# Moving four weight buffers by 32 bytes within each partition

## What is computed

```python
for i in range(DEPTH):
    h = rmsnorm(x, norm_mix_pre[i])
    m = ssd_mixer(h, ...) if i % 2 == 0 else rglru_mixer(h, ...)
    x = x + rmsnorm(m, norm_mix_post[i])
    h = rmsnorm(x, norm_ffn_pre[i])
    f = conv_ffn(h, ffn_w_up[i], ffn_conv_w[i], ffn_conv_b[i], ffn_w_down[i])
    x = x + rmsnorm(f, norm_ffn_post[i])
...
```

## Time and profile before

| what | before |
|---|---|
| median of 3 runs | 1814.41 us |
| the profiled execution's own time | 1813.63 us |
| its span, first to last instruction | 1811.3 us |
| TensorE matmul busy | 1763.0 us, 97% |
| TensorE weight load busy | 1642.5 us, 91% |
| VectorE busy | 1292.1 us, 71% |
| ScalarE busy | 1012.9 us, 56% |
| granted TensorE clock, mean | 0.997 of full speed |

### The profile page before, as it was taken

One profiled execution on the slowest core, in us unless ns is written; L12 is line 12 of the kernel. 1 busy time (PEld: TensorE's weight loads), 2 busy tenths in 40 slices (PEclk: granted clock), 3 DMA queues, 4 the chain that ended last, 5 costly groups with the idle time before them and its releaser, 6 DMA issues. The chain is left out here.

```text
span 1811.3 us, 37750 instructions
## 1 busy us (share of the span) xinstructions
PE 1763.0 (97%) x15197; PEld 1642.5 (91%) x15197; DVE 1292.1 (71%) x1997; ACT 1012.9 (56%) x1582; POOL 33.5 (2%) x56
## 2 busy tenths in 40 slices
PE   7999999999999999999999999999999999999999
PEld 7996788989979699899889999999998999999999
DVE  6838777777778987777778766775557876686555
ACT  6645565555576765555566654554455665455443
POOL 0000000000000000000000001000000000100000
PEclk9999999999999999999999999999999999999999
DMA  8540566677675565665636430545553542044553
GB/s 332 185 162 1 197 224 245 251 264 292 255 296 179 217 246 197 246 243 199 255 116 207 143 115 3 217 180 190 200 191 140 166 162 93 26 163 165 198 196 117
DMA packets 45285, 338.32 MB, mean 187 GB/s; under 512 B 5104, under 2 KB 5360, under 8 KB 6896
## 3 DMA queue, kind: packets, MB, share of 16 engines
q1 hardware_dynamic: 38736, 277.89, 42.8%
q0 software_dynamic: 4992, 52.43, 7.4%
q10 hardware_dynamic: 1440, 6.33, 0.9%
HBM read 333.48 MB, written 1.05 MB: 185 GB/s over the span
## 5 line engine op out<-in xcount | busy, mean ns | idle before, releaser
L679 DVE TENSOR_TENSOR w_lo<-raw,w_hi 128x1024 fp32r<-128x1024 f32 x526 | 638.7, 1224 | 355.0 <-ACT w_hi L670 341.4
L670 ACT ACTIVATE w_hi<-raw 128x1024 fp32r<-128x1024 f32 x526 | 553.4, 1060 | 547.0 <-PE unit L701 327.1
L699 PE MATMUL unit<-h_hi,w_hi 128*128 128x256 f32 x2528 | 705.7, 279 | 6.2 <-ACT keep L2028 1.9
L700 PE MATMUL unit<-h_lo,w_hi 128*128 128x256 f32 x2528 | 701.3, 277 | 0.0
L701 PE MATMUL unit<-h_hi,w_lo 128*128 128x256 f32 x2528 | 701.2, 277 | 0.0
L699 PEld LDWEIGHTS unit<-h_hi,w_hi 128*128 128x128 f32 x2528 | 476.1, 188 | 11.3 <-issue 3.2
L700 PEld LDWEIGHTS unit<-h_lo,w_hi 128*128 128x128 f32 x2528 | 474.9, 188 | 1.3
L701 PEld LDWEIGHTS unit<-h_hi,w_lo 128*128 128x128 f32 x2528 | 475.6, 188 | 0.0
L699 PE MATMUL acc<-mv_hi,w_hi 128*128 128x256 f32 x640 | 177.5, 277 | 0.4 <-DVE mv_lo L827 0.2
L700 PE MATMUL acc<-mv_lo,w_hi 128*128 128x256 f32 x640 | 177.3, 277 | 0.0
L701 PE MATMUL acc<-mv_hi,w_lo 128*128 128x256 f32 x640 | 177.3, 277 | 0.0
(11 more groups left out here) (420 smaller groups left out, 2127.8 us busy)
## 6 DMA issues: line engine op xcount, KB each, us to landing
raw<-w_in SPq DMA_DIRECT2D x263, 1024.0 KB, 4.8
ada_ring<-ada_in POOLq DMA_DIRECT2D x32, 1536.0 KB, 10.5
h<-rows_in ACTq DMA_DIRECT2D x5, 512.0 KB, 3.7
late<-keep POOLq DMA_DIRECT2D x8, 256.0 KB, 4.3
keep<-gates_in ACTq DMA_DIRECT2D x1, 1280.0 KB, 9.9
par<-par_in ACTq DMA_DIRECT2D x1, 1036.0 KB, 11.9
x<-x_in SPq DMA_DIRECT2D x2, 512.0 KB, 4.9
out<-x SPq DMA_DIRECT2D x4, 256.0 KB, 2.3
```

The costliest lines, as they stand in the source:

```text
L670: act(half(w_hi, c, k), raw[c % RAW][:, CW // 2 * k:CW // 2 * (k + 1)], ACT.Copy).then_inc(S("high_parts"), 1)
L679: tt(half(w_lo, c, k), raw[c % RAW][:, CW // 2 * k:CW // 2 * (k + 1)], half(w_hi, c, k).bitcast(f32), ALU.subtract).then_inc(S("chunk_spli ...
L699: mm(out, w, m, start=first, stop=False)
L700: mm(out, w, ml, start=False, stop=False)
```

## The change

The unused buffer ahead of the split weights grows from 84 to 92 words per partition. It occupied 352 bytes (84 words, rounded up to a multiple of 32) and occupies 384. The four buffers of split weights, and `late` with them, so lie 32 bytes higher: at 224 modulo 256 instead of 192. Everything that is placed before them, the activations among it, stays where it was. No instruction is added, taken away or moved.

```diff
         keep_cols, late_cols = 10752, 10240
         keep = sb("keep", [P, keep_cols])
-        sb("weights_offset", [P, 84])
+        sb("weights_offset", [P, 92])
         with nc.sbuf_tensor("late", [P, late_cols], f32) as late:
             pass
         w_hi = [sb(f"w_hi{i}", [P, CW], f32r) for i in range(2)]
```

## The result

Four runs of the changed kernel gave 1844.19 to 1849.65 us, median 1847.09. The kernel before, over four runs, has a median of 1816.04 us. The ratio is 1.0163, 95% interval 1.0137 to 1.0190, so the change costs about 30 us. Three later series of the kernel before, on three chips, had medians of 1821.11, 1823.27 and 1821.96 us; against those the cost would be 24 to 26 us. The forecast was 1824.5 us within 1799 to 1848; the direction was right, and the size lies next to the end that the forecast called all high.

What follows compares the result with a forecast made beforehand. TensorE's product pace was taken as the bound. The profiled 1813.6 us plus 10.1 for 256-column products, all other terms 0, gave 1823.7; with the median of the runs 0.8 higher, the forecast was 1824.5 us, range 1799 to 1848.

Steps and rivals of the forecast that it cites:

- all high: All 256-column products at the high pace of 117.8 ns: 33.1 us longer, 1847.5 us; far end of the forecast's own case.
- What bounds the kernel: TensorE's pace is the kernel's time, a product under way for 1763.0 of 1811.3 us; the splits follow it.
- Direction and range: Whole kernel: slower case 0.48, unchanged 0.22, faster 0.30; 1824.5 us, range 1799 to 1848 for 8 in 10.
- Two paces of one instruction, set by the distance between the operands: 256-column fp32r products run at 113.4 or 117.8 ns; moving stream and weight load lock, their address distance a plausible input.
- a pitch in no relation to them: Sign in TensorE's products: a pitch unrelated to 113.4 or 117.8 ns would prove the two-level picture too narrow.
- The 256-column term: About 10,460 TensorE products go from 28% to 50% at the high pace, 4.4 ns each: +10.1 us.
- The even deal: 256-column products at the new distance: both levels taken as evenly dealt, 50% high, since nothing is known of it.
- What lies between the fp32r pitch and the plain pass: 256-column products: 5.8 ns above 107.6 is a read conflict; a distance without it gains 60.7 us beyond 12.9.
- The 512-column term: The 1080 products with weights moving, 228 ns each: taken as 0, with 5 us left to the range.
- VectorE, ScalarE, `late`: Splits (1224 and 1060 ns) and loads of `late` (4.3 us) taken as unaffected by position: 0, `late` 1 us either way.
- the unchanged one: Rival: position doesn't matter, time rather than address decides each restart's level; 1814.4 us, chance 0.22.
- The faster one: Rival: restarts slide into the low pace everywhere, 12.9 us less, 512-column products perhaps 3 more; 1801.5 us, chance 0.30.

Runs made afterwards that it cites:

- all_up: Against the kernel before: activations and everything behind them, weights included, moved up 32 bytes, weights at 224, distance 64 as before; ratio 0.9985.
- mv_up: Against the kernel before: mv operands and everything behind them moved up 32 bytes, h stayed, so distance 96 for h and 64 for mv; ratio 1.0101.
- pair: Network left out, TensorE alone multiplying in bursts at various operand distances; 256-column pitch 119.8 ns at distance 0, 113.3 or 117.8 ns at 64.
- dist192: Against the kernel before: unused buffer of 116 words instead of 84, weights at 64 modulo 256, distance 192; 1848.9 us, ratio 1.0160.
- mod256: Against the kernel before: unused buffer of 20 words instead of 84, weights 256 bytes lower, distance again 64 modulo 256; ratio 0.9986.
- h_dist76: Against the kernel before: h_hi and h_lo start 244 bytes higher in longer buffers, at 116 modulo 256, weights 76 bytes behind; 1862.6 us, ratio 1.0219.
- h_dist52: Like the kernel with h at distance 76, but h_hi and h_lo at 140 modulo 256, weights 52 bytes behind; 1844.4 us, ratio 1.0123 to the kernel before.

## Why the prediction came out as it did

*What bounds the kernel*: right. TensorE's pace was the time; the 31.8 us found in the starts of its products are the 31.7 of the span, and no wait appeared.

*Direction and range*: right, and in part by luck. The slower side was chosen because seven tenths were low, not because anything was known of distance 96. And the same reasoning would have given the same range at any other place: at 0, 32, 128 and 192 the medians, 1865.6, 1853.1, 1857.7 and 1848.9 us, lie beyond its end of 1848.

*Two paces of one instruction, set by the distance between the operands*: right in its cause for positions in steps of 32, and shown by `all_up` and `mv_up`, which keep the weights at 224 and recover exactly the products whose distance goes back to 64. The number of paces was wrong: the forecast knew two, and named a pitch in no relation to them as what would prove its picture too narrow, which 119.9 ns at distance 0 does. The picture of two readers that lock to each other fits `pair`, where the bursts of most distances agree, but what is read when, and why 64 is good, stays a reading.

*The 256-column term, +10.1 us*: the step that was mis-sized. I took the new distance as one at which 113.4 and 117.8 ns are dealt evenly. The trace had shown these two levels in the big groups at one distance only, and they belong to that distance. Every other multiple of 32 has its own one or two levels, all between 116.7 and 120.0 ns but for one of eight bursts at 192 (113.3) and a few short stretches of `dist192`; at 96 they average 117.7. The term measured 29.0 us by the starts of products, or (280.2 - 277.4) x 10,460 = 29.3 by the durations. The all-high bound of 33.1 us held, but not as a bound: distance 0 went past it, with 119.9 ns. Part of the 29.0 is where I started from: the profiled execution had 72% of its products low, and stands near the fast end of the 1812.8 to 1832.8 us over which this kernel spreads. The even deal is what distance 64 itself gives in other executions: in the profiles of `all_up` and `mod256` the mean pitch is 115.4 and 115.2 ns, about halfway, where it was 114.7.

*What lies between the fp32r pitch and the plain pass*: not borne out. I read the 5.8 ns above 107.6 as a conflict that a better distance could remove. None of the 64 distances went under 113.3 ns, nor did quarter-width stationary tiles. So nothing here gives any of the 60.7 us on the fast side, nor all of the 12.9: no distance in steps of 32 had the low pace in every burst.

*The 512-column term, 0 with 5 us either way*: +5.9 us, just outside. Among these, too, the distance tells the pace, by a table of their own, and they moved from a good place (229.1 ns at 192) to an ordinary one (233.3 at 160).

*VectorE, ScalarE, `late`*: right. 1224 and 1058 ns against 1224 and 1060; the loads of `late` land in 4.4 us against 4.3, and the rest of TensorE's time went down by 3.1 us, not up.

*The rivals*: the unchanged one had time as the only cause and fell with the result, and again with five more distances that each cost over 1%. The faster one fell too: its case was that 28% high was much, and it turned out that the other places in steps of 32 have hardly anything low at all.

The trace of before did hold one more sign that I passed over. `pe_tokens_unit` ran weights against activations at distance 192 and was never low, 117.8 ns throughout. That was a second distance in the same trace, and it pointed to the low pace as the exception. With it the even deal would have been hard to defend.

On the rule that TensorE's two read ports are independent (the Trainium skill, "TensorE: Matmul & The Clock Gate", section "Step-by-step: what each phase is for"): the measurements decide against it for fp32r, as far as the pace goes. The same products cost 113.3 to 120.0 ns as only the distance of the two operands changes. The 16-byte cachelines of the Trainium skill's page "SBUF — State Buffer", section "Door 1: The DMA port swizzle (why `[64,N]` ≈ `[32,N]`)", could bear on `h_dist76` and `h_dist52`, whose moving tiles begin off a multiple of 16, at 116 and 140. For the stationary tile alone they are no bar to the best pace: at distances 52 and 76 it begins at 180 and 204, off a multiple of 16, and holds 113.3 ns. For the moving tile no run here separates lines from the rest.

## What to carry to other kernels

When TensorE is the bound, compute the pitch of its products from their starts, and move one operand by 32 bytes at a time through all eight places: it costs one line each, and here the places are up to 2.4% apart. Two pitches in one form say that there is something to look for, not that another place is better; here the place with these two pitches was the best of the seven tried. Record the distance between the operands, not a buffer's own address, and re-check it whenever a buffer is inserted between them, since an innocent change of size ahead of the weights does what this change did. A microbenchmark of the product stream gives the table at once, as long as it puts both operands where the kernel will have them: the one here had the moving tile at 128, and was wrong for moving tiles at 116 and 140.

## What the runs showed of the hardware that was not expected

The pace of a 256-column fp32r product changes as the stationary operand moves by 4 bytes, by up to 8% (113.3 to 122.2 ns, in one burst 123.2), with no other engine at work. For operands at multiples of 32 the distance modulo 256 told the levels in every case tried, of which one was a shift by 256. Plain fp32 products of the same size keep a pitch of 215.7 to 215.9 ns (L1853) in all twelve kernels with the network, also in `all_up` and `mv_up`, where `con` lies 32 bytes further from `h`.

Distance 64 makes a kernel whose runs differ among themselves: the kernels with it gave 1812.8 to 1832.8 us, those at 0, 128 or 192, with four executions each, stay within 3 us each. The profiles show where it comes from: the first MLP is at 113.4 ns in the profile of the kernel before and at 117.8 in those of `all_up` and `mod256`. The spans of these two are 5.7 and 12.6 us longer than that of before, and the starts of their products give 5.8 and 12.4. The clock is not it: executions of the kernel before took 1814.6 and 1828.9 us, both with a mean granted clock of 0.996. That the paces explain the slowest executions as well, which have no profile, was not tested. The fastest place is therefore also the least steady one.
